# Expert loop: the scatter of the last pair between the two halves of the gate and up products, the picks' transposes ahead of the gated products' transposes

## What is computed

```python
group_prob = softmax(xf @ w_rg + b_rg)                  # 4 groups
grp = argmax(group_logits)
top_logit, top_local = top_k(expert_logits[grp], 2)     # 2 of the 8 experts of that group
gates = p_grp * softmax(top_logit)
# for every expert e of 32, for the tokens that chose it:
y = (silu(xb @ w_gate[e]) * (xb @ w_up[e])) @ w_down[e]
out[token] += gate * y
```

## Time and profile before

| what | value |
|---|---|
| median of 3 runs | 1985.64 us (1985.08, 1985.64, 1987.7) |
| profiled execution, its own time | 1982.81 us |
| its span, first to last instruction | 1981.0 us |
| mean granted TensorE clock | 0.988 of full speed |
| TensorE busy | 1890.3 us (95%) |
| VectorE, ScalarE, GpSimd busy | 755.9 (38%), 614.6 (31%), 267.6 us (14%) |
| gate and up products, L2071 and L2073 together | 2048 products, about 0.6 us each, two side by side |
| scatter products, L2045 | 240, 393 ns each (median), issued every 0.24 us or so |
| HBM read | 555.11 MB, mean 281 GB/s |

### The profile page before, as it was taken

How to read it: one execution, slowest core, us unless ns; L and a number is a source line. 1 busy time by engine, 2 the same in 40 slices (tenths; PEclk the granted TensorE clock), 3 DMA queues, 4 the chain that set the end, 5 groups by cost and what they waited for, 6 DMA issues and landing times.

```text
span 1981.0 us, 27126 instructions
## 1 busy us (share of the span) xinstructions
PE 1890.3 (95%) x10968; PEld 1245.4 (63%) x10968; DVE 755.9 (38%) x1751; ACT 614.6 (31%) x1178; POOL 267.6 (14%) x247
## 2 busy tenths in 40 slices
PE   8999999999998999999999999999999989999997
PEld 6764444444446754444444446888889968788996
DVE  3333122211212333122111214556665644756665
ACT  2312111111112312111111113456555444574653
POOL 1400000000000400000000003871000057600000
PEclk9999999999999999999999999999999999999999
DMA  9458999999998357999999995452435744433353
GB/s 364 155 195 336 416 427 427 428 428 429 428 413 296 132 206 327 419 427 427 428 429 429 428 424 199 156 205 76 153 101 170 263 141 168 168 128 104 114 177 117
DMA packets 121423, 557.50 MB, mean 281 GB/s; under 512 B 5008, under 2 KB 49584, under 8 KB 96240
## 3 DMA queue, kind: packets, MB, share of 16 engines
q1 hardware_dynamic: 119696, 551.51, 70.4%
q10 hardware_dynamic: 1440, 4.36, 0.6%
q0 software_dynamic: 192, 0.30, 0.1%
HBM read 555.11 MB, written 1.05 MB: 281 GB/s over the span
## 4 chain that ended last, share of the span: by engine, by line
PE 84%; DMA 6%; ACT 4%; DVE 4%; issue 2%; POOL 0%; SPq 0%; POOLq 0%; DVEq 0%
PE bank L2071 14%; PE bank L2102 10%; PE bank L1822 7%; DMA ring<-w_up_dram 6%; PE bank L2073 6%; PE bank L1831 4%; PE bank L2216 3%; PE bank L2218 3%; PE bank L2217 3%; PE bank L2195 3%; PE bank L2196 3%; PE bank L2197 3%; PE bank L1814 3%; PE bank L1910 3%; PE bank L2274 3%; PE bank L2045 3%
## 5 line engine op out<-in xcount | busy, mean ns | idle before, releaser
L2071 PE MATMUL bank<-ring,work 128*64 128x512 f32 x544 | 242.5, 601 | 10.6 <-issue 10.6
L2073 PE MATMUL bank<-ring,work 128*64 128x512 f32 x512 | 230.6, 605 | 0.0
L758 POOL TENSOR_TENSOR w_lo<-ring,w_hi 128x512 fp32r<-128x512 f32 (+1 forms) x160 | 208.6, 1324 | 78.7 <-ACT w_hi L954 76.4
L1472 DVE TENSOR_TENSOR work<-work,bank 64x512 f32<-64x512 f32 x64 | 43.9, 686 | 446.0 <-ACT work L909 446.0
L714 POOL TENSOR_TENSOR stat<-stat,power 128x1 f32<-128x1 f32 (+1 forms) x18 | 10.8, 602 | 1493.0 <-DVE stat L1116 1457.9
L909 ACT ACTIVATE work<-bank 64x512 f32<-64x512 f32 x64 | 37.9, 592 | 472.4 <-PE bank L2073 472.4
L954 ACT CAST w_hi<-ring 128x512 fp32r<-128x512 f32 (+1 forms) x208 | 123.3, 606 | 130.8 <-PE bank L2218 86.9
L2102 PE MATMUL bank<-ring,work 128*64 128x512 f32 x480 | 155.8, 595 | 1.8 <-ACT work L914 0.4
L2071 PEld LDWEIGHTS bank<-ring,work 128*64 128x64 f32 x544 | 73.1, 138 | 122.3 <-issue 120.4
L1691 DVE TENSOR_TENSOR w_lo<-ring,w_hi 128x512 fp32r<-128x512 f32 (+1 forms) x176 | 116.1, 678 | 79.3 <-ACT w_hi L1067 79.1
L1822 PE MATMUL bank<-hT,ring 128*128 128x256 f32 x640 | 143.6, 379 | 0.0
(11 more groups left out here) (326 smaller groups left out, 4089.0 us busy)
## 6 DMA issues: line engine op xcount, KB each, us to landing
ring<-w_in_dram SPq DMA_DIRECT2D x34, 2048.0 KB, 8.4
ring<-w_gate_dram SPq DMA_DIRECT2D x34, 2048.0 KB, 20.6
ring<-w_up_dram SPq DMA_DIRECT2D x32, 2048.0 KB, 26.1
ring<-w_down_dram SPq DMA_DIRECT2D x30, 2048.0 KB, 25.6
ring_tail<-w_down_dram SPq DMA_DIRECT2D x18, 2048.0 KB, 23.6
work<-w_gate_dram SPq DMA_DIRECT2D x16, 2048.0 KB, 19.1
work<-w_up_dram SPq DMA_DIRECT2D x16, 2048.0 KB, 25.9
ring_tail<-w_up_dram SPq DMA_DIRECT2D x16, 2048.0 KB, 27.1
```

Source lines behind the costliest of these rows:

```text
L758: pool.tensor_tensor(w_lo[:, g % CHUNKS, 0:n], w[:, k], w_hi[:, g % CHUNKS, 0:n], ALU.subtract).then_inc(chunk_lo, 1)
L2071: pe.matmul(m_bank(m)[gate, :], lhs, wg[:, k], start=(k == 0), stop=(k == KD - 1), skip_group_check=True)
L2073: mu = pe.matmul(m_bank(m)[up, :], lhs, wu[:, k], start=(k == 0), stop=(k == KD - 1), skip_group_check=True)
```

## The change

The call of `scatter(p - 1)` moves from behind the second half of the gate and up products to between the two halves. The T_COMB section moves ahead of the T_HID section. Nothing is added or removed: every instruction, operand and bank stays, and no other engine's program changes. TensorE's queue in a pair becomes: gather, first half, scatter of the last pair, second half, T_COMB, T_HID, down products. The first pair of a layer (`first and p == 0`) has no scatter.

```diff
--- before.py
+++ after.py
@@ -2073,15 +2073,8 @@
                                 mu = pe.matmul(m_bank(m)[up, :], lhs, wu[:, k], start=(k == 0), stop=(k == KD - 1),
                                                skip_group_check=True)
                             m_done(mu, m)
-                        if p > 0 or not first:
-                            scatter(p - 1)
-                        m = m0 + T_HID
-                        m_claim(m)
-                        m_emptied(m0 + T_GU)
-                        m_emptied(m0 + T_GU + 1)
-                        for f in range(FE):
-                            mm = pe.transpose(m_bank(m)[:, f * P:(f + 1) * P], hid[:, f * P:(f + 1) * P], ident[:])
-                        m_done(mm, m)
+                            if side == 0 and (p > 0 or not first):
+                                scatter(p - 1)
                         m = m0 + T_COMB
                         m_claim(m)
                         pe.wait_ge(M["gated"], i * 4 + (p + 1))
@@ -2090,6 +2083,13 @@
                         for t in range(NT):
                             mm = pe.matmul(m_bank(m)[:, SEQ:SEQ + 2], pick[:, b, t], pair_gates[:, b, t],
                                            start=(t == 0), stop=(t == NT - 1))
+                        m_done(mm, m)
+                        m = m0 + T_HID
+                        m_claim(m)
+                        m_emptied(m0 + T_GU)
+                        m_emptied(m0 + T_GU + 1)
+                        for f in range(FE):
+                            mm = pe.transpose(m_bank(m)[:, f * P:(f + 1) * P], hid[:, f * P:(f + 1) * P], ident[:])
                         m_done(mm, m)
                         m_claim(m0 + T_OUT)
                         m_claim(m0 + T_OUT + 1)
```

## The result

The changed kernel takes 2030.08 us (median of six runs, 2027.5 to 2036.51) against 1985.69 us: a ratio of 1.0228, 95% interval 1.0209 to 1.0247. The direction was forecast, the size was not: 44 us instead of 13, and the time lies outside the range. The profiled execution of the changed kernel has a span of 2028.4 us, 47.4 us more than before's 1981.0. The medians differ by 44.4 us, because the profiled execution of the kernel before, at 1982.81 us, lies 2.9 us under its median.

What follows compares the result with a forecast made beforehand. The weight stream bounds both expert loops now; with the change TensorE would, end to end. The pairs' extra less the room gave 6.8 + 6.6 = 13.4 us, so 1999.0 us against the median 1985.64; range 1992.5 to 2006.5 us.

Steps and rivals of the forecast that it cites:

- The bound and the room: Expert loops: the weight stream sets the end; TensorE has 18.4 us of room over layer 0's 15 pairs, 1.23 a pair.
- The room theory: Expert loops: extra TensorE work up to 1.23 us a pair is hidden by the weight stream; only the excess lengthens them.
- The queue's price: TensorE's queue in a pair: the moved scatter adds 1.75 us in the first turn, 1.66 us in the loop.
- My upper bound: Extra for a pair: at most 1.85 us, if both waits in the loop wake as late as the first turn's.
- The falls of the clock: TensorE in both expert loops: granted clock forecast to stay at 1.00, so no cost for falls in the sum.
- the third rival: Clock falls in the gaps before the down products, in a third of 30 pairs: 16.5 us more, 2015.5 us; chance 9%.
- The rule of the Trainium skill: Transposes don't count as busy for the clock gate; by it the 2.7 us looks empty, falls frequent, 16.5 us or more.
- The stream: Weight loads in the loops: up to 1.6 us lost once a layer, last down piece landed by 592.5 us, at no cost.
- The first rival: The stream hides the scatter in the wait for second-half weights if a pair's extra is at most 1.20 us; chance 6%.
- The partly hidden case: Some 0.3 us of a pair's extra is not there: 1.35 us a pair, 3.8 us in all, 1989.4 us; chance 5%.

Runs made afterwards that it cites:

- comb_only: Kernel before with only T_COMB moved ahead of T_HID, the scatter still behind the second half; 1987.09 us, ratio 1.0010.
- half_fill0: Changed kernel with four scatter products between the halves, four behind, plus twelve filler transposes in pair 0 of each layer; 1983.72 us, ratio 0.9994.
- before_fill10: Kernel before with ten filler products ahead of T_HID in the 15 pairs of a layer with a scatter; 2017.38 us, ratio 1.0163.
- filled kernels: Four versions of the changed kernel with throwaway products or transposes in one or both of TensorE's idle gaps; 2000.49 to 2002.32 us.
- scatter_only: Kernel before with only the scatter moved between the halves, T_HID still ahead of T_COMB; 2026.2 us, ratio 1.0201.
- half_scatter: Changed kernel with the scatter split, four products between the halves and four behind the second half; 1986.71 us, ratio 1.0012.
- fill_transposes: Changed kernel with filler transposes in both idle gaps, seven ahead of T_COMB's transposes and five behind T_HID's; 2000.49 us, ratio 1.0074.

## Why the prediction was wrong, step by step

**The bound and the room: right.** The kernel before has 18.4 us of room in a layer because the stream is slower than TensorE's own pace. Under the room, `comb_only` (0.62 us a pair) and `half_fill0` (0.97) cost 0.1% and nothing; over it, `before_fill10` costs its 67 us of queue less 36.9. The room theory was precise to a few us, apart from the soft edge above.

**The queue's price: right in mechanism, over a quarter too small in what is left after the room.** I had 1.75 and 1.66 us a pair. Measured: 28.87 - 27.02 and 28.77 - 26.92, 1.85 us each. Two terms were mis-sized. The gap between the halves is 303.70 to 306.28, 2.58 us, and not 2.49: the 64-wide products start 0.09 us later behind the scatter than the transposes did. And T_HID starts 0.14 us behind VectorE's end (314.73 to 314.87), as in pair 0, where I took the 0.05 us of a wait in the loop. My upper bound was 1.85 us, but made of two late wake-ups; one came, and the longer break took the place of the other, so that it held is in part luck. Each of the small differences is multiplied by 30 and nothing of it disappears in the room: 18.5 us instead of 13.4. Alone it would have given 1985.7 + 18.5 = 2004, inside the range. The filled kernels show it: their loops are 18.4 to 19.0 us longer than before's, and their times 2000.5 to 2002.3 us.

**The falls of the clock: the step that failed.** They were the third rival, at 9% and 16.5 us. The sum had them at nothing ("the granted clock at 1.00 through both loops"). They came 17 times and cost 28.7 us, which carried the time out of the range. What misled me was the argument that pair 0 has this very sequence and kept its clock in both layers. It isn't quite this sequence, for in the kernel before T_HID comes first there, and TensorE stands still once for 1.51 us and then for 0.21. And two cases were too few. Seven of the kernels, the kernel before among them, have pair 0 with neither scatter nor filler, so 14 such stretches stand in their profiles, and behind six of them the clock fell: once in the changed kernel, twice in `scatter_only`, twice in `half_scatter`, once in `before_fill10`. That is three of the eight with T_HID first and three of the six with T_COMB first. The clock falls behind such a stretch about every other time, in pair 0 as elsewhere, and two cases could not tell that from never. The measured size of the rival is 17 of 32 pairs, where I had put a third of 30 at 9%. The other row should have weighed more: the kernel before has eight waits for weights of 2.16 to 2.26 us, and six of them, three in each layer, were followed by a fall within 1.0 us.

**The rule of the Trainium skill** ("TensorE: Matmul & The Clock Gate", Part 4, PE-mode transpose) pointed the right way, but for a reason that this case contradicts. By it transposes don't count as activity, and the fillers of `fill_transposes` could have changed nothing. They took away all the falls, as the products did: 2000.49 against 2001.44 us. The measurement decides: with fp32 transposes of 128 x 128 in the gaps the clock stayed at 1.00 in both loops. The profile lists them as MATMUL and doesn't show in which mode the array ran them.

**The stream: right in outcome, wrong in its bound.** The last weights landed at 597.1 and not by 592.5. Two falls in the first turn delayed the issues on which I had put 1.6 us at most: the stream brought 348 GB/s in pair 2 (DMA share 0.86, shown above), where `fill_transposes`, without the falls, has

```profile
196.79:225.66 28.87, 28.61 (x174) 13.60 (x175) 5.35 (x15) 3.73 (x6) 0.00 (x0) 1.00 0.97 399
```

and lands its last weights at 591.3. It cost nothing, since the products wanted them at 615.7.

**The first rival** needed at most 1.20 us a pair; at 1.85 it was out. `comb_only` and the split scatter show that it would have held below that. The partly hidden case was out too: no term was cheaper by more than 0.01 us, two were dearer.

## What to carry to other kernels

Work that fills the wait of one engine for another is worth more than its duration: taken away, it leaves the wait, and here two waits of 0.7 to 0.8 us in one quiet stretch of TensorE were followed by half clock in half of the pairs, at 1.7 us each, more than the waits themselves. Where a reordering leaves TensorE standing in places, price the clock as its own term, with about an even chance where this case is the only measure, or fill the gap with throwaway products or transposes, which cost at most 0.02 us a pair in these waits. Where a stream of weights is the bound, compute the room a pair has before counting anything, and put the extra work ahead of the last wait for weights, not behind it.

## What the runs showed of the hardware

The falls come in groups. In the changed kernel they follow two to four pairs in a row, then three pairs in a row have none (the first six in layer 1), though the stretches ahead of them are the same (312.78 and 463.40 above). What decides between the two isn't shown. The number of falls seems to change from one execution to the next: the six runs of the changed kernel go from 2027.5 us at a mean clock of 0.980 to 2036.5 us at 0.976, and 0.4% of the span is 8 us. That would also be why its spread is wider than that of the filled kernels (1999.1 to 2003.1 for all four).

A wait in the first turn, which is unrolled, and in the run-time loop is not the same. The down products start 0.14 us behind ScalarE's copy in the first turn and 0.05 us in the loop, in every pair of both kernels. T_HID's start behind VectorE's product is 0.14 to 0.15 us in both parts of the changed kernel, and in pair 0 of the kernel before.
